# Moving part of two modulation products from TensorE beside a convolution to VectorE inside two feed-forward loops

## The reference

```
# first_block: layers 1 and 2 (mixers: state space with attention; conformer convolution)
mod = silu(c) @ mod_w[layer] + mod_b[layer]
sh1, sc1, g1, sh2, sc2, g2 = split(mod, 6)
# second_block: layers 3 and 4 (mixers: latent attention, MLA; Hyena)
mod_x = silu(c_2) @ mod_w_2[i] + mod_b_2[i]
mod_c = silu(c_ctx_2) @ mod_w_2[i] + mod_b_2[i]      # of layer 3 only shift 1 and scale 1 are used
hx = rmsnorm(x, norm_mix_g[i]) * (1 + sc1) + sh1
x = x + g1 * mixer(hx)                               # MLA takes its keys from the context too, by mod_c
h = rmsnorm(x, norm_ffn_g[i]) * (1 + sc2) + sh2
z = dwconv3(h @ w_up); a, g = split(z, 2)
x = x + g2 * ((silu(g) * a) @ w_down)
```

## Time and profile before

| | us |
|---|---|
| median of three runs | 1529.02 (1528.15 to 1534.12) |
| span of the profiled execution | 1526.8 |
| PE busy (matmuls) | 1429.8, 94% |
| DVE busy | 1128.1, 74% |
| ACT busy | 772.9, 51% |
| DMA, whole span | 315.65 MB, 207 GB/s |

### The profile page before, as it was taken

One profiled execution on the slowest core, in us unless ns is written; L12 is line 12 of the kernel. 1 busy time (PEld: TensorE's weight loads), 2 busy tenths in 40 slices (PEclk: granted clock), 3 DMA queues, 4 the chain that ended last, 5 costly groups with the idle time before them and its releaser, 6 DMA issues.

```text
span 1526.8 us, 24920 instructions
## 1 busy us (share of the span) xinstructions
PE 1429.8 (94%) x9483; PEld 1193.0 (78%) x9483; DVE 1128.1 (74%) x1680; ACT 772.9 (51%) x1090; POOL 51.5 (3%) x38
## 2 busy tenths in 40 slices
PE   5498989999999999999999889999999999999998
PEld 1385568899976668999979655799997877799997
DVE  7999746988884457999984476686667858776666
ACT  3322356555563365555554666564546542455554
POOL 2600200000000000000001000000000000000000
PEclk9898999999999999999999999999999999999999
DMA  9332945988869766988734401355545433345551
GB/s 359 134 129 90 347 162 197 354 318 306 313 242 390 303 230 252 353 342 334 287 147 138 125 0 48 115 186 192 192 170 191 162 111 138 111 169 189 185 196 59
DMA packets 58060, 315.65 MB, mean 207 GB/s; under 512 B 7011, under 2 KB 8524, under 8 KB 33856
## 3 DMA queue, kind: packets, MB, share of 16 engines
q1 hardware_dynamic: 53826, 303.30, 53.8%
q10 hardware_dynamic: 4158, 11.30, 2.3%
HBM read 311.85 MB, written 1.15 MB: 205 GB/s over the span
## 4 chain that ended last, share of the span: by engine, by line
PE 75%; DVE 13%; ACT 5%; issue 4%; DMA 2%; ACTq 0%; SPq 0%; DVEq 0%; POOL 0%
PE bank L2232 62%; DVE w_lo L1339 2%; PE bank L2491 2%; ACT w_hi L751 1%; PE bank L2575 1%; PE bank L2106 1%; PE bank L2124 1%; PE bank L2183 1%; DMA arena<-in_mod_later 1%; PE bank L2300 1%; ACT hf L1256 1%; DVE h_lo L1541 1%; DVE hf L1553 1%; ACT hf L793 1%; DVE hf L1993 1%
## 5 line engine op out<-in xcount | busy, mean ns | idle before, releaser
L1339 DVE TENSOR_TENSOR w_lo<-raw,w_hi 128x2048 fp32r<-128x2048 f32 x186 | 426.2, 2292 | 169.6 <-ACT w_hi L751 168.4
L2232 PE MATMUL bank<-h_hi,w_hi 128*128 128x256 f32 x1800 | 517.3, 287 | 11.3 <-DVE h_lo L1541 9.7
L2232 PE MATMUL bank<-h_lo,w_hi 128*128 128x256 f32 x1800 | 510.8, 284 | 0.0
L2232 PE MATMUL bank<-h_hi,w_lo 128*128 128x256 f32 x1800 | 510.7, 284 | 0.0
L751 ACT ACTIVATE w_hi<-raw 128x2048 fp32r<-128x2048 f32 x186 | 355.8, 1915 | 129.8 <-PE bank L2232 114.6
L2232 PEld LDWEIGHTS bank<-h_hi,w_hi 128*128 128x128 f32 x1800 | 347.1, 193 | 21.3 <-DVE h_lo L1541 11.9
L2232 PEld LDWEIGHTS bank<-h_lo,w_hi 128*128 128x128 f32 x1800 | 347.0, 193 | 2.3 <-issue 0.7
L2232 PEld LDWEIGHTS bank<-h_hi,w_lo 128*128 128x128 f32 x1800 | 346.7, 193 | 0.0
L1756 DVE SCALAR_TENSOR_TENSOR arena<-bank,par,arena 128x255 f32<-128x255 f32 (+1 forms) x264 | 109.1, 475 | 111.5 <-ACT arena L988 79.1
L2232 PE MATMUL bank<-w_hi,a_hi 128*128 128x512 f32 x368 | 145.8, 396 | 4.9 <-DVE a_lo L1781 4.0
L2232 PE MATMUL bank<-w_hi,a_lo 128*128 128x512 f32 x368 | 144.3, 392 | 0.0
(11 more groups left out here) (327 smaller groups left out, 1703.5 us busy)
## 6 DMA issues: line engine op xcount, KB each, us to landing
raw<-in_stream SPq DMA_DIRECT2D x186, 1024.0 KB, 5.0
arena<-in_mod_stream SPq DMA_DIRECT2D x64, 768.0 KB, 7.5
arena<-in_mod_later SPq DMA_DIRECT2D x48, 512.0 KB, 8.0
raw<-in_mod_pe SPq DMA_DIRECT2D x36, 512.0 KB, 6.6
arena<-in_mod_pe SPq DMA_DIRECT2D x12, 512.0 KB, 12.7
sq<-row_store ACTq DMA_DIRECT2D x7, 512.0 KB, 3.5
sq<-in_bias SPq DMA_DIRECT2D x8, 256.0 KB, 6.7
x<-in_x_t ACTq DMA_DIRECT2D x1, 1024.0 KB, 8.6
```

The source lines that it names most:

```text
L1339: nc.vector.tensor_tensor(w_lo[s][:], raw[s][:], w_hi[s][:].bitcast(F32), ALU.subtract).then_inc(lo_done, 1)
L2232: ins = nc.tensor.matmul(out_, l, r, start=first and n == 0, stop=last and n == 2, **kw)
```

## The change

Layer 3's pieces are cut to the first 16 (shift 1 and scale 1, which the context needs too). The other four vectors of layer 3 and the first two of layer 4 are now the 16 blocks of `ffn(1)`; the last four of layer 4 are 11 new blocks (`LAST_BLOCKS`, the last padded with zeros) in `ffn(2)`, one before the loop and one in each step, in four slots. Pieces 0 to 7 stand where the fifth group stood, pieces 8 to 15 behind the projection instead of the sixth. Their turns move into `ffn(1)`, behind `first_up_gate`. PE adds up the new blocks (`mod_turn(2, ...)`) between `ffn(2)` and Hyena. `stay_awake` goes from 12 to 4 ahead of `ffn(1)` and from 14 to 2 behind `ffn(2)`. `later_out`, `mod_out`, `rows_turn`, `store_rows` and `load_gate` move to where the new order has their inputs. SP gets two waits of its own: all pieces used ahead of `ffn(1)`'s loads, and all blocks of `ffn(2)` used behind its loads. The core of the diff:

```diff
+LAST_BLOCKS, LAST_SLOTS = 11, 4
+LATER_PIECES = 16
...
+        last_keep = at(FREE, LAST_BLOCKS * MOD_COLS)
+        last_w = mod_w[0:START_SLOTS] + [at(FREE + LAST_BLOCKS * MOD_COLS, DT // 2, MOD_COLS)]
...
-        MB = {1: 0, 4: MOD_BLOCKS}
+        MB = {0: 0, 1: MOD_BLOCKS, 2: 2 * MOD_BLOCKS}
+        MOD_PER = {0: 3, 1: 3, 2: 2}
+        MOD_PLAN = {3: ({0: 1, 2: 2}, {0: 3}), 2: ({0: 1}, {0: 2}), None: ({}, {})}
...
-        LATER_AFTER = (0, 3, 5, 6)
+        LATER_SUM = (3, 6)
...
@@ SP @@
-            load_plain("cm_in", 1, 2)
-            load_later(0, 5)
-            load_plain("cm_in", 2, 3)
+            load_plain("cm_in", 1, 4)
             sp.wait_ge(sem("taps_turned"), 4)
             sp.wait_ge(sem("mod_used"), MOD_SLOTS + 2 * MOD_BLOCKS)
...
-            load_later(32, 40)
             load_plain("cm_out", 3)
-            load_later(40, 48)
-            load_ffn(1, MB[4])
+            load_later(12, LATER_PIECES)
+            sp.wait_ge(sem("later_used"), LATER_PIECES)
+            load_ffn(1)
...
-            load_ffn(2, None)
+            load_ffn(2)
+            sp.wait_ge(sem("hy_hid"), 2)
+            sp.wait_ge(sem("mod_used"), MOD_SLOTS + 4 * MOD_BLOCKS + 2 * LAST_BLOCKS)
...
@@ ACT @@
+            later_copy(0)
+            projection_norm("cm_out", 4, gate=3, aux=1)
+            later_copy(1)
+            ffn(1, 8)
...
@@ DVE @@
+            def later_out():
+
+                dve.wait_ge(sem("later_turned"), 2)
+                bias = par[:, COL["mod_b_2"]:COL["mod_b_2"] + 16]
+                nc.vector.tensor_tensor(mod[:, 3, 0:16], bank[6][:, T:T + 16], bias, ALU.add)
+                nc.vector.tensor_tensor(mod[:, 2, 0:16], bank[6][:, T + 64:T + 80], bias, ALU.add).then_inc(sem("later_out"), 1)
+                dve.wait_ge(sem("later_out"), 1)
...
-            mod_out(4, 32, "mod_b_2")
+            mod_out(0, [(3, 16, 48), (4, 0, 16)])
...
-            ffn(2, 3, None, None)
+            ffn(2, 8)
             norm_x(12)
+            mod_out(1, [(4, 16, 48)])
...
@@ PE @@
-                stay_awake(12)
+                stay_awake(4 if f == 1 else 12)
...
+                if f == 1:
+                    pe.wait_ge(sem("later_copied"), 2)
+                    later_turn(0)
+                    later_turn(1)
...
-                if c in LATER_AFTER:
-                    g = LATER_AFTER.index(c)
-                    later(8 * g, 8 * g + 8)
...
-            later(32, 36)
+            later(0, 4)
...
-                    later(36, 40)
-            projection("cm_out", h_of(LAYER_NORM), [(1, lambda: later(40, 48)), (2, lambda: later_turn(5))])
-            rows_turn(2)
+                    later(4, 8)
+            projection("cm_out", h_of(LAYER_NORM))
+            later(8, LATER_PIECES)
+            pe.wait_ge(sem("later_copied"), 1)
             ffn(1)
...
-            stay_awake(14, 5)
+            mod_turn(2, range(LAST_BLOCKS))
+            stay_awake(2, 5)
             x_turn(12, 1, 5)
```

More of the change, by code:

```diff
@@ L386, in build @@
         hy_w = [at(20224 + HY_HID * i, HY_HID)[0:n, :] for i, n in enumerate((33, HY_HID))]
-        angle = [at(11264 + T * i, T)[0:HY_HID, :] for i in range(2)]
+        angle = [at(14848 + T * i, T)[0:HY_HID, :] for i in range(2)]
         hy_cols = sb("hy_cols", [P, 6])
@@ L460, in build @@
             MOD_HALF.append((mod_w[key], mod_landed[key], _n_[key], MOD_SLOTS))
+        for m in range(2 * LAST_BLOCKS):
+            key = m % LAST_SLOTS
+            _n_[key] += 16
+            MOD_HALF.append((last_w[key], mod_landed[key], _n_[key], LAST_SLOTS))
         pm_landed = [sem(f"piece_landed{i}") for i in range(PM_SLOTS)]
@@ L581, in load, with load_mod @@
                 sp.dma_start(raw[s][:], src).then_inc(raw_landed[s], 16)
-            def load_mod(m, i=None):
-                more = 0 if i is None else 6 * i
+            def load_mod(m, i=None, per=3):
+                more = 0 if i is None else 2 * per * i
                 buf, landed, _, n = MOD_HALF[m]
@@ L841, in norm_x, with projection_norm @@
                     x_square(n, j, BY_TOKENS)
-            def projection_norm(name, n, late=False, gate=None, aux=None):
+            def projection_norm(name, n, gate=None, aux=None):
                 hi_upto(Q[name] + 3)
@@ L1033, in run @@
                             hi(nq + k, i)
-                        if b0 is not None and k in blocks:
+                        if k in blocks:
                             mod_begin(b0 + blocks[k], i)
@@ L1057, in ffn @@
                 nxt[0] = q0 + 35
[L1059 removed]
+            ffn(0)
             def later_copy(g):
                 act.wait_ge(sem("later_used"), 8 * g + 8)
[L1064 to L1066 removed]
+                nc.scalar.activation(later_acc[g], half(LATER_SUM[g], 0), ACT.Copy).then_inc(sem("later_copied"), 1)
             act.wait_ge(sem("cm_landed"), 64)
@@ L1295, in _ @@
                 hi_upto(q + 3)
+                if j == 3:
+                    store_rows(3)
                 if j in HY_WINDOW:
@@ L1790, in run @@
                             lo(nq + k, i)
-                        if b0 is not None and k in blocks:
-                            mod_block(b0 + blocks[k], c0, i)
+                        if k in blocks:
+                            mod_block(b0 + blocks[k], c0, i, blocks_per)
                 g = step(0, q0)
@@ L2145, in x_turn, with mod_turn @@
                         ins.then_inc(sem("x_turned"), 1)
-            def mod_turn(b0, blocks, dst=6):
+            def mod_turn(f, blocks):
+                keep = mod_keep if f == 1 else last_keep
                 for b in blocks:
-                    pe.wait_ge(sem("mod_used"), MOD_SLOTS + 2 * (b0 + b) + 2)
+                    pe.wait_ge(sem("mod_used"), MOD_SLOTS + 2 * (MB[f] + b) + 2)
                     for n in range(3 * b, 3 * b + 3):
-                        ins = nc.tensor.matmul(bank[dst][:, n:n + 1], mod_keep[:, n * P:(n + 1) * P], ones[:, 0:1], start=True, stop=True)
+                        ins = nc.tensor.matmul(bank[6][:, n:n + 1], keep[:, n * P:(n + 1) * P], ones[:, 0:1], start=True, stop=True)
                     ins.then_inc(sem("mod_turned"), 1)
@@ L2559, in later_turn @@
                 pe.wait_ge(sem("later_copied"), g + 1)
-                for i in range(2 if g < 2 else 1):
+                for i in range(2):
                     for n in range(2):
                         c = T + 64 * i + 8 * g + n
-                        ins = nc.tensor.matmul(bank[3][:, c:c + 7:2], later_acc[g % 2][:, n * P:(n + 1) * P], ident[:, i:P:32],
+                        ins = nc.tensor.matmul(bank[6][:, c:c + 7:2], later_acc[g][:, n * P:(n + 1) * P], ident[:, i:P:32],
                                                start=True, stop=True)
```

155 lines of the change are left out of this document (76 added, 79 removed).

## The result

The changed kernel takes 1559.16 us in the median of four runs (1556.33 to 1560.18) against 1529.69: a ratio of 1.0186, 95% interval 1.0168 to 1.0203. It is slower, as forecast, but by 29.5 us where 15.3 were forecast, and the time lies 1.2 us above the range.

What follows compares the result with a forecast made beforehand. TensorE (PE), 75% of the chain, was taken as the bound in most stages. −22.9 + 1.0 + 13.7 + 1.6 + 3.0 + 4.6 + 0 + 10.3 + 4.0 = +15.3; 1526.8 + 15.3 + 2.2 = 1544.3 us, range 1528 to 1558.

Steps and rivals of the forecast that it cites:

- The clock and the columns: End of ffn2: 33 column matmuls and 2 fillers cost +4.0 beyond the room; low clock after PE's idle wait costs 1.5.
- Part A: Convolution: modulation pieces and PE's wait for them leave the chain, −22.9 us; a later bias row gives back +1.0.
- the new wait: Convolution: PE, arriving about 10 us earlier, may wait for the residual's bias row, +1.0 us (0 to 5).
- Part C: Start of ffn2: PE waits twice for low halves behind blocks, 2.0 and 2.6 late, together +4.6 us (3 to 7).
- Part D: Loop of ffn2: eleven blocks bring DVE to 94% while PE stays busy, 0 us (0 to +5).
- rival (d): Loop of ffn2: DVE becomes the bound, +15 us, giving 1559; chance 0.09.
- Part E: End of ffn2: the held first Hyena chunk delays the last down product, +10.3 us (8.5 to 13); column sums add +4.0.
- Part B: Start of ffn1: first weight chunk held until pieces are used, then a serial chain, +13.7 us; +15.2 with its clock.
- The turns: In ffn1, behind the first up and gate chunks: two turns of the kept groups, +1.6 us.
- (a): Start of ffn1: the wait ahead of it costs nothing, giving 1529, no change; chance 0.10.
- (b): End of ffn2: the wait there costs nothing because DVE is ahead, giving 1532.5; chance 0.08.
- Rival (c): Start of ffn1 and end of ffn2: neither wait binds, giving 1517, faster; chance 0.08.

Runs made afterwards that it cites:

- e1: Changed kernel with SP's wait for used pieces moved from ahead of ffn1's first weight chunk to ahead of its first modulation half: 1543.62 us, ratio 1.0101.
- e2: Changed kernel with Hyena's first three chunks loaded ahead of SP's wait for all eleven blocks: 1549.4 us, ratio 1.0136.
- e3: Changed kernel with both the e1 and e2 edits: 1528.77 us, ratio 0.9998.
- e4: Changed kernel with 60 matmuls of zeros on PE ahead of ffn2's last down product: 1558.14 us, ratio 1.0188.
- e5: e3 with the 33 column matmuls moved behind Hyena's first two chunks and 14 fillers again: 1533.25 us, ratio 1.0034.
- e8: e3 with DVE's addition of the bias row to x moved behind the first gated product and next low half: 1521.55 us, ratio 0.9956.
- e10: e12 with e8's edit and ffn2's odd-step blocks behind the up chunk's low half: 1515.23 us, ratio 0.9915.
- e13: e3 with one filler behind each block's three column matmuls instead of two behind all: 1532.76 us, ratio 1.002.
- e12: e3 with the first five blocks' column sums ahead of ffn2's last down product, six behind it: 1523.94 us, ratio 0.9968.

## Why the prediction was wrong

The sign and the mechanism of the two waits were right: two waits of SP hold back a chunk on which three engines' programs depend, and e1, e2 and e3 show them as 15.5, 9.8 and together 30.4 us. What was wrong is the price of the column sums and of the clock around them, and several smaller terms erred to the same side. The sum was short by 15.0, in these terms and with 0.4 at the very end, less the 1.7 that the changed kernel was ahead before anything had changed.

- **The clock and the columns (5.7 short).** The step that failed is the one that took 0.217 us for each of the 33 column matmuls, from a row at full clock, and 1.5 us for the clock of that place. Columns and fillers took 11.1 us (10.27 of it the columns) and not 7.15 + 0.4, so they cost 7.5 beyond the room of 3.6, for the +4.0 forecast. The last down product took 2.5 more than 5.6 and the transposes up to Hyena 1.25 more, 3.7 for 1.5. I had laid all of the clock to the idle wait. e4 shows that only the down product's part is that: with PE busy through the wait the product is 2.4 shorter, but from its start to Hyena's first matmul it is 23.3 us for 24.3, and the kernel's time is the same. e5 shows that the rest comes with the columns, since it moves with them. The column sums had no bounds in the forecast at all. The trace of before had the fall, in the windows right at and behind the row that I used, and with e1 it shows that it doesn't always come (two rows of before, then the two of the same code in e1):

```profile
802.00:805.00 3.00, 3.00 (x29) 3.00 (x29) 1.15 (x3) 2.71 (x5) 0.00 (x0) 1.00 0.00 0
805.00:808.00 3.00, 3.00 (x22) 3.00 (x22) 2.88 (x2) 3.00 (x5) 0.00 (x0) 0.76 0.00 0
...
785.00:788.00 3.00, 3.00 (x29) 3.00 (x28) 1.02 (x4) 2.85 (x4) 0.00 (x0) 1.00 0.00 0
788.00:791.00 3.00, 3.00 (x26) 3.00 (x26) 3.00 (x2) 3.00 (x4) 0.00 (x0) 1.00 0.00 0
```

The price of one instruction was read, and not the stretch behind it, where the clock is 0.76 with PE busy for all 3 us.

- **Part A (3.2 short).** The gain was right, as e8 shows; the new wait was priced at 1.0 within 0 to 5. It was 3.47 us in the changed kernel, and 1.9 to 5.6 in the profiled runs that lack e8's edit, and the six matmuls behind it took up to 2.8 us more at the lower clock (5.33 in e2 for 2.57 in e8). "What the row queued behind is what goes" was the wrong reason for the near end: the row still took 9.1 us to land after its issue (470.51 to 479.60), and in before 11.2. PE came 9.5 us earlier (480.7 for 490.2), the row 7.0.

- **Part C (2.8 short).** The two waits stand where I put them, with 3.07 and 2.35 us for 2.0 and 2.6. The rest, 2.0 of 7.4, lies in the steps up to the next few chunks and isn't resolved to rows here. The loop itself costs nothing: DVE is busy for 155.84 of 177 us, 88% where 94% was forecast, PE for 128.00 of 128 us from 1030 to 1158, and the low halves keep their distance from those of before from the fifth step on. Part D is right, and rival (d) falls; that the time it named, 1559, is the one that came is chance.

- **Part E (2.4 short).** The held chunk takes 9.01 us behind three tables of 512 KB, and I had 1172.2 − 1165.2 = 7.0 for it; the bound was 1175, and 1180.60 is 1174.6 there once the 6.0 are taken off by which `ffn2` runs later. The rest of the serial chain is as listed.

- **Part B** (+16.0 for 15.2) is right in each step, to within 0.8 us together. The clock, which I counted as a loss, is 0.50 from 560 to 576, and the first eight transposes take 1.97 us, in e1 0.87.

- **`ffn1` to `ffn2` (1.4 short).** The turns cost 1.69 us, as forecast. The rest differs from run to run: between the first two `uq` chunks the changed kernel loses 1.6 us on the one before, e1 wins 1.5, and e3 does neither, with the same code there. It goes with the clock behind the same 15 columns: 0.50 from 802 to 808 in the changed kernel, 0.76 and then 0.67 from 805 to 811 in the one before, 1.00 in e1. The 1.7 us ahead of the convolution, where nothing was changed, differ from run to run too.

Rivals (a), (b) and (c) fall for the kernel as it is. Rival (c) named the kernel that e3 makes, 1517, and e3 took 1528.77: without the two waits the terms of C, of the columns and of their clock still take back all of A. (The 22.9 stand against 11.2 at other places by the prediction's own terms, 1.0 + 1.6 + 4.6 + 4.0, and not 5.6; the 1517 has all four.)

The range failed with the sum. The forecast's bounds, to 1553, hold only where the terms' errors partly cancel; the upper bounds that it gives for the single terms come to 1563.7 when all are added, and the errors of A, B, C, E and the columns all went that way.

The Trainium skill's "TensorE: Matmul & The Clock Gate", section "Why this matters for your kernels", asks for no long idle gaps of PE between bursts of matmuls. The trace agrees on such gaps: the clock is 0.50 behind both waits. But keeping PE busy through one of them, in e4, brought nothing that the runs can tell (1558.14 for 1559.16); at the end of `ffn2` the fall that cost more came at a PE that was not idle.

## What to carry to other kernels

A wait that is put on a queue of loads for the sake of one buffer holds everything behind it: put it just ahead of the load that needs it, and let what needs it least go first. When work is added to a tuned loop, look at its last turn and the first turn: a block that costs nothing in the loop stood twice on the chain at its start and once at its end. And when a price is read from a row, read the clock of the stretch behind it too.

## What was not expected of the hardware

Behind matmuls with one moving column (128 x 128 weights each) the granted clock often falls from 1.00 to 0.50, its lower level, at a PE that is busy for 3.00 of 3 us: in the kernel before (0.76 in the window from 805 to 808), the changed one (1194 to 1203), e5, e10 to e13. Wherever 33 of them stand in one row, with or without fillers, it falls while they run. Behind 15 of them it falls in some executions and not in others of the same code: before has 0.76 from 805 to 808, e1 1.00 from 788 to 791; the down product behind 15 takes 5.66 us in e12 and 7.79 in e10. What decides stays open here. A filler of 512 columns behind each three of them did not hold the clock. What came behind them ran at half speed: eight transposes 1.71 us for 0.87, eight filter matmuls 7.04 for 3.63.
